# The probabilities of the latent attention turned by VectorE, and its output one group later

## The chip, the cores and the metric

The kernel runs on one core of a Trainium2 chip. The metric is device time in microseconds (us) of one launch. The kernel before takes 2406.18 us, the median of three runs (2406.07 to 2406.28).

## The reference, cut to what matters

Two transformer blocks over a sequence of 256 tokens of width 2048, in float32. The second block has three attention branches (A, B and C); each is multiplied by a SiLU gate, projected to width 2048, multiplied by a sigmoid gate, and the three are summed. The change is in branch B, a latent attention with 8 heads. A head has queries and keys of 192 features (128 plain ones and 64 rotated ones) and values of 128:

```python
logits = jnp.einsum('bthd,bshd->bhts', qb, k) * 192 ** -0.5
logits = jnp.where(causal, logits, -jnp.inf)        # 128 queries at a time
p = jax.nn.softmax(logits, axis=-1)
o_b = jnp.einsum('bhts,bshd->bthd', p, v)           # then times silu(bz)
```

The last product sums over the keys. On TensorE the summed dimension lies on the partitions, so the probabilities, whose partitions are the queries, have to be turned before it. With two blocks of 128 queries and causal masking, a head has three squares of 128x128 probabilities: 384 columns.

## The kernel before, in words

**The weight stream.** All weights come from one stream of 841 groups of 512 KB, two tiles of 128x512 each. A group passes a ring of four slots (`RING`): SyncE's queue loads it into `RAW`, ScalarE copies it to `WH` (the high part, line 1165), VectorE computes `WL = RAW - WH` (the low part, line 1722), and TensorE multiplies it in twelve matmuls of 128x512 (lines 682 to 684): high by high, high by low, low by high, for two tiles and two halves of the tokens. ScalarE's split of group j waits until TensorE has used group j-4 (`group_used`), VectorE's waits for ScalarE's (`hi_split`), TensorE's matmuls wait for VectorE's (`lo_split`), and the load of a slot waits for the low split of the group that was in it.

**Order on an engine.** Each engine runs one list of instructions in order; engines wait for one another by semaphores. The functions named `b_step(i, p)` exist on TensorE, ScalarE and VectorE and say what that engine does for the attention after group p of a merge. ScalarE and VectorE do the split of group p+4 first and then the step of p; with p in `ahead` (ScalarE, line 1341) or a function `first` (VectorE, line 1955), something comes before that split.

**The stage.** `merge_a` runs four times 12 groups: eight of a gate's weights and four of branch A's projection. Beside each 12 groups it computes two heads of branch B, a pair i = 0 to 3. ("Group 5" is group 5 of the twelve; "split 9" the split of group 9, which is issued at step 5.) The steps of a pair are:

- TensorE at step 4: the scores of the pair (`pair_scores`, lines 1082 and 1087), in PSUM banks 6 and 7.
- VectorE at step 4, after split 8: scaled and masked scores `BSC` (line 2363) and the negated maxima (2365, 2366).
- ScalarE at step 5, after split 9: a load of the activation table and four exponentials into `BPR` (1678), with their sums.
- TensorE at step 7: six transposes of `BPR` through the identity into PSUM banks 4 and 5 (`pair_probs`, line 1095). ScalarE at step 7 copies them to `BPT` (1683).
- TensorE at step 8: the values' products from `BPT` (`pair_values`, 1104). VectorE at step 8: the gated rows `BOF` (2369, 2373).
- At step 10: TensorE turns `BOF` (`pair_output`, 1112), ScalarE copies the high part to `U[2]` (1686), VectorE subtracts the low part (2380) and counts `head_out`.
- VectorE at steps 7 to 10, after that step's split: 4, 2, 4 and 2 transposes of 32x384 of the next pair's normed and rotated queries and keys `BQK` into `BQT` (`pair_turn`, 2348), and 2 each at the next pair's steps 0 and 1. The first pair's are done by TensorE.
- ScalarE at step 2, after split 6: two gain scalings of `BQT` (1667, 1668), which release that pair's scores (`qkt_ready`).
- VectorE at step 11: the gated product is multiplied and added to the sum (1974, 1977).
- GpSimd prepares `BQK` of the next pair (lines 640 to 660), from the end of the transposes of `BQK` on.

Branch A's attention runs in the merge before (`merge_c`), one head to six groups. There VectorE turns the probabilities already, with sixteen transposes of 32x96 ahead of the split of the head's group 2 (`probs_turn`, line 1838), and the exponentials are ScalarE's step 1.

Of the kernel before, what the change touches and what calls it, by code (L numbers as in the profile page):

```python
# [25 lines left out]
ACT = mybir.ActivationFunctionType  # L26
# [3 lines left out]
P = 128  # L30
# [13 lines left out]
NCH = D // CH  # L44
# [5 lines left out]
CAUS = 3 * P  # L50
# [21 lines left out]
MOBA0, RET0, C0, A0, B0, HEADS = 0, 8, 12, 16, 24, 28  # L72
# [109 lines left out]
def build(nc, x_in, mem_in, w_stream, params, final_w, pos_pack, constants, out):  # L182
    with ExitStack() as ctx:
# [29 lines left out]
        MERGED = {"merged1": sb("MERGED1", [P, T, D], F32, at_pb), "merged2": sb("MERGED2", [P, T, D], F32, at_pa + 20 * KB)}  # L213
# [46 lines left out]
        BPR = sb("BPR", [P, 2, CAUS], F32, at_sgx + 8 * KB)  # L260
        BPT = sb("BPT", [P, 2, CAUS], F32, at_sgx + 11 * KB)
# [23 lines left out]
        PS = ctx.enter_context(nc.psum_tensor("PS", [P, 8, 512], F32))  # L285
# [20 lines left out]
        ident = con("ident")  # L306
# [53 lines left out]
        probs = sem("probs")  # L360
        probs_scaled = sem("probs_scaled")
        v_copied = sem("v_copied")
        pt_done = sem("pt_done")
        pt_ready = sem("pt_ready")
# [301 lines left out]
        def _(pe):  # L666
# [421 lines left out]
                                        start=False, stop=t == T - 1, skip_group_check=True)  # L1088
                ins.then_inc(scores, 1)

            def pair_probs(H):
                pe.wait_ge(probs, H.count(1))
                for r in range(2):
                    for b in range(3):
                        ins = pe.transpose(PS[:, 4 + r, b * P:(b + 1) * P], BPR[:, r, b * P:(b + 1) * P], ident)
                ins.then_inc(pt_done, 1)

            def pair_values(H, i):
                pe.wait_ge(pt_ready, H.count(1))
                for r in range(2):  # L1100
# [14 lines left out]
            def b_step(i, p):  # L1115
                H = At(B0, i, 1)
                if p == 1 and isinstance(i, int):
                    pair_transpose(H)
                elif p == 4:
                    pair_scores(H)  # L1120
                elif p == 7:
                    pair_probs(H)
                elif p == 8:
                    pair_values(H, i)
                elif p == 10:
                    pair_output(H)
            products("gates_b1", [(GD, HT)], 0)
            products("merge_a", [(GD, HT), (GW, U[1])], 0, b_step)
# [7 lines left out]
            g, n = At(GROUP0["out2"]), At(PROD0["out2"] + NCH - 1)  # L1136
# [19 lines left out]
        def _(act):  # L1156
# [140 lines left out]
            for p in range(GD - 1, 2 * GD):  # L1297
# [7 lines left out]
                if p in (GD, GD + 1):  # L1305
# [4 lines left out]
                    ins = act.activation(JUNK[:, t, :], X[:, t, :], ACT.Square, scale=D ** -0.5, accum_out=XR[:, t:t + 1])  # L1310
# [13 lines left out]
            for a in range(2):  # L1324
                act.activation(ROPE[:, 1, a], ANG[:, 0], ACT.Sin)
                ins = act.activation(ROPE[:, 0, a], ANG[:, 1], ACT.Sin, scale=-1.0, bias=con("hpi"))
# [336 lines left out]
            def b_step(i, p):  # L1663
                H = At(B0, i, 1)
                if p == 2 and not isinstance(i, int):
                    act.wait_ge(qk_tr, H.count(2))
                    act.activation(BQT[:, 0:2, :], BQT[:, 0:2, :], ACT.Copy, scale=par("bqn"))
                    act.activation(BQT[:, 2:4, :], BQT[:, 2:4, :], ACT.Copy, scale=par("bkn")).then_inc(qkt_ready, 1)
                elif p == 2:
                    act.wait_ge(qk_tr, H.count(2))  # L1670
                    act.activation(BQT[:, 0:2, :], PS[:, 4, :].rearrange("p (r s) -> p r s", r=2), ACT.Copy, scale=par("bqn"))
                    act.activation(BQT[:, 2:4, :], PS[:, 5, :].rearrange("p (r s) -> p r s", r=2), ACT.Copy, scale=par("bkn"))
                    act.activation(BQT[:, 4:6, :], PS[:, 6, :].rearrange("p (a s) -> p a s", a=2), ACT.Copy).then_inc(qkt_ready, 1)
                elif p == 5:
                    act.wait_ge(maxima, At(20, i, 1).count(1))
                    for t, cols in enumerate((slice(0, P), slice(P, CAUS))):
                        for r in range(2):
                            ins = act.activation(BPR[:, r, cols], BSC[:, r, cols], ACT.Exp, bias=BNM[:, t, r:r + 1],
                                                 accum_out=BRS[:, t, r:r + 1])
                    ins.then_inc(probs, 1)  # L1680
                elif p == 7:
                    act.wait_ge(pt_done, H.count(1))
                    act.activation(BPT[:], PS[:, 4:6, 0:CAUS], ACT.Copy).then_inc(pt_ready, 1)
                elif p == 10:
                    act.wait_ge(ot_done, H.count(1))
                    act.activation(U[2][:, ds(i * 2, 2), 0, :], PS[:, 7, :].rearrange("p (r s) -> p r s", r=2),
                                   ACT.Copy).then_inc(ot_hi, 1)
            merge("merge_a", NCH, 1, 0, b_step, apart=1)
            act.wait_ge(head_out, HEADS + 1)
            act.dma_start(X[:], rows(x_scratch)).then_inc(x_back, 16)  # L1690
            gates_b("gates_b", 2, 2)
# [22 lines left out]
        def _(dve):  # L1714
# [638 lines left out]
            def b_step(i, p):  # L2353
                H = At(B0, i, 1)
                own, ahead = not (isinstance(i, int) and i == 0), not (isinstance(i, int) and i == NCH - 1)
                if own and p < 2:
                    pair_turn(H, 6 + p)
                if ahead and 7 <= p < 11:
                    for h in ((0, 1), (2,), (3, 4), (5,))[p - 7]:
                        pair_turn(At(B0 + 1, i, 1), h)  # L2360
                if p == 4:
                    dve.wait_ge(scores, H.count(1))
                    link(dve.scalar_tensor_tensor(out=BSC[:], in0=PS[:, 6:8, 0:CAUS], scalar=192 ** -0.5,
                                                  in1=con("mask").unsqueeze(1).broadcast_to([P, 2, CAUS]), op0=ALU.mult, op1=ALU.add))
                    dve.tensor_reduce(BNM[:, 0], BSC[:, :, 0:P], AX_X, ALU.max, negate=True)
                    dve.tensor_reduce(BNM[:, 1], BSC[:, :, P:CAUS], AX_X, ALU.max, negate=True).then_inc(maxima, 1)
                elif p == 8:
                    dve.wait_ge(probs, H.count(1))
                    link(dve.reciprocal(BRI[:], BRS[:]))
                    dve.wait_ge(pv_done, H.count(1))  # L2370
                    for r in range(2):
                        for t in range(T):
                            ins = dve.scalar_tensor_tensor(out=BOF[:, r, t], in0=PS[:, 6, r * S + t * P:r * S + (t + 1) * P],
                                                           scalar=BRI[:, t, r:r + 1], in1=PB[:, t, ds((i * 2 + r) * P + PB_Z, P)],
                                                           op0=ALU.mult, op1=ALU.mult)
                    ins.then_inc(o_rows, 1)
                elif p == 10:
                    dve.wait_ge(ot_hi, H.count(1))
                    u = U[2][:, ds(i * 2, 2)]
                    dve.tensor_tensor(u[:, :, 1, :], PS[:, 7, :].rearrange("p (r s) -> p r s", r=2), u[:, :, 0, :].bitcast(F32),  # L2380
                                      ALU.subtract).then_inc(head_out, 1)
            merge("merge_a", NCH, 1, MERGED["merged2"], 2, b_step, apart=True)
            for p in range(2 * GD):
                split(At(GROUP0["gates_b"]), p + RING)
            dve.wait_ge(prod_free, 2 + PROD0["up_b"])
# [134 lines left out]
```

## Time and profile before

| what | value |
|---|---|
| median of 3 runs | 2406.18 us |
| the profiled execution | 2406.36 us |
| its span, first to last instruction | 2404.5 us |
| TensorE busy | 2397.9 us (100%) |
| VectorE busy | 1837.5 us (76%) |
| ScalarE busy | 1235.8 us (51%) |
| GpSimd busy | 320.2 us (13%) |
| granted TensorE clock | 1.00 |

The stage `merge_a` lies at about 2076 to 2229 us of the span. All rows below are of this one execution; times are us from the span's start. Engines: PE is TensorE, DVE VectorE, ACT ScalarE, POOL GpSimd. L1722 is line 1722 of the kernel. A matmul's duration contains the drain of the array; the next one starts before it ends, so the time that a series takes on the path is read from starts.

### The profile page before, as it was taken

The numbers are of one execution on the slowest core, as the hardware profiler recorded it, in microseconds if no ns is written. First come the engines' busy times: TensorE is split into PE (matmuls) and PEld (weight loads), VectorE is DVE, ScalarE is ACT, GpSimd is POOL, SyncE is SP. The second block draws the span as 40 slices with busy tenths as digits, with TensorE's granted clock in tenths as the row PEclk, the third lists the DMA queues.
The fourth block names the chain that finished last, engine by engine and source line by source line (L and its number), as shares of the span: only waits on it lengthen the run. The fifth ranks groups of instructions, "written<-read, shape, count | busy, mean of one in ns | idle before, by whom it ended". The sixth has DMA issues, their size and how long they took to land.

```text
span 2404.5 us, 34078 instructions
## 1 busy us (share of the span) xinstructions
PE 2397.9 (100%) x10821; PEld 1983.1 (82%) x10821; DVE 1837.5 (76%) x2616; ACT 1235.8 (51%) x1585; POOL 320.2 (13%) x277
## 2 busy tenths in 40 slices
PE   9999999999999999999999999999999999999999
PEld 7888888888888888888888888888888888888887
DVE  5467679897888988988888897667767876587584
ACT  5445455555455444444444455455557555655443
POOL 0021242234210000000000000011100000521050
PEclk9999999999999999999999999999999999999999
DMA  7555555576655655555565656855554555555655
GB/s 272 193 186 178 178 177 175 184 245 226 228 185 185 203 196 192 191 193 191 185 199 192 198 188 213 253 184 187 171 187 161 182 166 180 179 167 167 227 193 166
DMA packets 134828, 464.25 MB, mean 193 GB/s; under 512 B 14545, under 2 KB 21329, under 8 KB 134113
## 3 DMA queue, kind: packets, MB, share of 16 engines
q1 hardware_dynamic: 122464, 443.08, 56.2%
q10 hardware_dynamic: 12256, 20.15, 2.7%
q8 instruction: 45, 0.74, 0.1%
q14 instruction: 31, 0.25, 0.0%
q0 software_dynamic: 32, 0.03, 0.0%
HBM read 455.87 MB, written 7.34 MB: 193 GB/s over the span
## 4 chain that ended last, share of the span: by engine, by line
PE 96%; DVE 2%; issue 1%; ACT 1%; DVEq 0%; ACTq 0%
PE PS L682 21%; PE PS L684 21%; PE PS L683 21%; PE PS L929 7%; PE PS L930 7%; PE PS L931 7%; PE PS L949 3%; PE PS L951 3%; PE PS L950 3%; DVE WL L1722 1%; DVE PT L1838 1%; PE PS L798 1%; PE PS L767 1%; PE PS L723 0%; PE PS L1104 0%
## 5 line engine op out<-in xcount | busy, mean ns | idle before, releaser
L1165 ACT ACTIVATE WH<-RAW 128x1024 fp32r<-128x1024 f32 x841 | 889.6, 1061 | 1087.1 <-PE PS L684 693.8
L1722 DVE TENSOR_TENSOR WL<-RAW,WH 128x1024 fp32r<-128x1024 f32 x811 | 1020.7, 1267 | 485.9 <-ACT WH L1165 475.5
L682 PE MATMUL PS<-WH,HT 128*128 128x512 f32 (+1 forms) x1816 | 716.0, 394 | 0.3 <-DVE WL L1722 0.2
L684 PE MATMUL PS<-WH,HT 128*128 128x512 f32 (+1 forms) x1816 | 706.2, 389 | 0.0
L683 PE MATMUL PS<-WL,HT 128*128 128x512 f32 (+1 forms) x1816 | 705.5, 388 | 0.0
L682 PEld LDWEIGHTS PS<-WH,HT 128*128 128x128 f32 x1816 | 341.1, 188 | 71.9 <-issue 3.7
L684 PEld LDWEIGHTS PS<-WH,HT 128*128 128x128 f32 x1816 | 340.9, 188 | 70.9
L683 PEld LDWEIGHTS PS<-WL,HT 128*128 128x128 f32 x1816 | 341.2, 188 | 67.8
L929 PE MATMUL PS<-WH,HT 128*128 128x512 f32 x704 | 274.0, 389 | 0.0
L931 PE MATMUL PS<-WH,HT 128*128 128x512 f32 x704 | 273.9, 389 | 0.0
L930 PE MATMUL PS<-WL,HT 128*128 128x512 f32 x704 | 273.9, 389 | 0.0
L2119 DVE STREAM_TRANSPOSE FU<-PS 32x256 f32<-32x256 f32 x352 | 156.9, 446 | 6.0
L931 PEld LDWEIGHTS PS<-WH,HT 128*128 128x128 f32 x704 | 132.1, 188 | 27.5
L929 PEld LDWEIGHTS PS<-WH,HT 128*128 128x128 f32 x704 | 132.1, 188 | 27.4
L930 PEld LDWEIGHTS PS<-WL,HT 128*128 128x128 f32 x704 | 132.1, 188 | 27.4
L949 PE MATMUL PS<-WH,ACTT 128*128 128x512 f32 x352 | 136.9, 389 | 0.0
L950 PE MATMUL PS<-WL,ACTT 128*128 128x512 f32 x352 | 136.9, 389 | 0.0
L951 PE MATMUL PS<-WH,ACTT 128*128 128x512 f32 x352 | 136.9, 389 | 0.0
L682 PE MATMUL PS<-WH,U 128*128 128x512 f32 x320 | 127.7, 399 | 0.0
L684 PE MATMUL PS<-WH,U 128*128 128x512 f32 x320 | 124.8, 390 | 0.0
L683 PE MATMUL PS<-WL,U 128*128 128x512 f32 x320 | 124.5, 389 | 0.0
L488 POOL TENSOR_TENSOR MS<-MS,CONST 128x4 f32<-128x4 f32 (+1 forms) x6 | 1.2, 200 | 916.8 <-ACT PS L1206 744.3
(320 smaller groups left out, 2328.4 us busy)
## 6 DMA issues: line engine op xcount, KB each, us to landing
RAW<-w_stream SPq DMA_DIRECT2D x841, 512.0 KB, 3.4
bias_scratch<-BE ACTq DMA_DIRECT2D x12, 256.0 KB, 4.1
MEMR<-mem_in ACTq DMA_DIRECT2D x1, 2048.0 KB, 10.8
X<-x_in ACTq DMA_DIRECT2D x4, 512.0 KB, 4.3
x_scratch<-X ACTq DMA_DIRECT2D x4, 512.0 KB, 4.4
X<-x_scratch ACTq DMA_DIRECT2D x1, 2048.0 KB, 11.7
out<-X ACTq DMA_DIRECT2D x8, 256.0 KB, 3.2
X<-x_in SPq DMA_DIRECT2D x3, 512.0 KB, 9.9
```

What stands on the lines that cost most here:

```text
L682: pe.matmul(o, hi, WH[:, slot, kk, 0:cols], start=k == 0, stop=False)
L683: pe.matmul(o, hi, WL[:, slot, kk, 0:cols], start=False, stop=False)
L684: ins = pe.matmul(o, lo, WH[:, slot, kk, 0:cols], start=False, stop=k == nq * GK - 1)
L929: pe.matmul(o, hi, WH[:, slot, kk, :], start=k == 0, stop=False)
L930: pe.matmul(o, hi, WL[:, slot, kk, :], start=False, stop=False)
L931: ins = pe.matmul(o, lo, WH[:, slot, kk, :], start=False, stop=k == KT - 1)
L949: pe.matmul(o, hi, WH[:, slot, kk, :], start=k == 0, stop=False)
L950: pe.matmul(o, hi, WL[:, slot, kk, :], start=False, stop=False)
L951: ins = pe.matmul(o, lo, WH[:, slot, kk, :], start=False, stop=k == FT - 1)
L1165: act.activation(WH[:, g.slot(j)], RAW[:, g.slot(j)], ACT.Copy).then_inc(hi_split, 1)
L1722: dve.tensor_tensor(WL[:, s], RAW[:, s], WH[:, s].bitcast(F32), ALU.subtract).then_inc(lo_split, 1)
L2119: ins = dve.transpose(dst, src)
```

## The change: what it does

For each pair of heads the six TensorE transposes of the probabilities and ScalarE's copy of them go. VectorE turns the probabilities instead, from `BPR` straight to `BPT`, in sixteen transposes of 32x192 (32 partitions by six blocks of 32) ahead of its split of step 5 (that of group 9). On ScalarE the exponentials of step 5 stand ahead of that step's split. The output's three parts move from step 10 to step 11. TensorE adds one to the semaphore `pt_done` after the scores, so that its count stays right.

```diff
--- before.py
+++ after.py
@@ -1088,13 +1088,6 @@
                                         start=False, stop=t == T - 1, skip_group_check=True)
                 ins.then_inc(scores, 1)
 
-            def pair_probs(H):
-                pe.wait_ge(probs, H.count(1))
-                for r in range(2):
-                    for b in range(3):
-                        ins = pe.transpose(PS[:, 4 + r, b * P:(b + 1) * P], BPR[:, r, b * P:(b + 1) * P], ident)
-                ins.then_inc(pt_done, 1)
-
             def pair_values(H, i):
                 pe.wait_ge(pt_ready, H.count(1))
                 for r in range(2):
@@ -1118,11 +1111,10 @@
                     pair_transpose(H)
                 elif p == 4:
                     pair_scores(H)
-                elif p == 7:
-                    pair_probs(H)
+                    pe.sem_inc(pt_done, 1)
                 elif p == 8:
                     pair_values(H, i)
-                elif p == 10:
+                elif p == 11:
                     pair_output(H)
             products("gates_b1", [(GD, HT)], 0)
             products("merge_a", [(GD, HT), (GW, U[1])], 0, b_step)
@@ -1678,14 +1670,11 @@
                             ins = act.activation(BPR[:, r, cols], BSC[:, r, cols], ACT.Exp, bias=BNM[:, t, r:r + 1],
                                                  accum_out=BRS[:, t, r:r + 1])
                     ins.then_inc(probs, 1)
-                elif p == 7:
-                    act.wait_ge(pt_done, H.count(1))
-                    act.activation(BPT[:], PS[:, 4:6, 0:CAUS], ACT.Copy).then_inc(pt_ready, 1)
-                elif p == 10:
+                elif p == 11:
                     act.wait_ge(ot_done, H.count(1))
                     act.activation(U[2][:, ds(i * 2, 2), 0, :], PS[:, 7, :].rearrange("p (r s) -> p r s", r=2),
                                    ACT.Copy).then_inc(ot_hi, 1)
-            merge("merge_a", NCH, 1, 0, b_step, apart=1)
+            merge("merge_a", NCH, 1, 0, b_step, apart=1, ahead=(5,))
             act.wait_ge(head_out, HEADS + 1)
             act.dma_start(X[:], rows(x_scratch)).then_inc(x_back, 16)
             gates_b("gates_b", 2, 2)
@@ -2374,12 +2363,23 @@
                                                            scalar=BRI[:, t, r:r + 1], in1=PB[:, t, ds((i * 2 + r) * P + PB_Z, P)],
                                                            op0=ALU.mult, op1=ALU.mult)
                     ins.then_inc(o_rows, 1)
-                elif p == 10:
+                elif p == 11:
                     dve.wait_ge(ot_hi, H.count(1))
                     u = U[2][:, ds(i * 2, 2)]
                     dve.tensor_tensor(u[:, :, 1, :], PS[:, 7, :].rearrange("p (r s) -> p r s", r=2), u[:, :, 0, :].bitcast(F32),
                                       ALU.subtract).then_inc(head_out, 1)
-            merge("merge_a", NCH, 1, MERGED["merged2"], 2, b_step, apart=True)
+
+            def b_turn(i, p):
+                H = At(B0, i, 1)
+                if p == 5:
+                    dve.wait_ge(probs, H.count(1))
+                    for a in range(4):
+                        for b in range(4):
+                            src = BPR[32 * a:32 * a + 32].rearrange("p r (n s) -> p (r n) s", s=P)[:, :, 32 * b:32 * b + 32]
+                            dst = BPT[32 * b:32 * b + 32].rearrange("p r (n s) -> p (r n) s", s=P)[:, :, 32 * a:32 * a + 32]
+                            ins = dve.transpose(dst, src)
+                    ins.then_inc(pt_ready, 1)
+            merge("merge_a", NCH, 1, MERGED["merged2"], 2, b_step, apart=True, first=b_turn)
             for p in range(2 * GD):
                 split(At(GROUP0["gates_b"]), p + RING)
             dve.wait_ge(prod_free, 2 + PROD0["up_b"])
```

## Rows read from the trace of the kernel before

**Rows 1.** Busy time in 38 us of the second pair: us of each engine (instructions), clock, DMA

```profile
core 0: us, PE busy (x) PEld busy (x) DVE busy (x) ACT busy (x) POOL busy (x), PEclk, DMA share, GB/s
2116.00:2154.00 38.00, 38.00 (x186) 31.36 (x185) 30.76 (x40) 20.46 (x28) 12.47 (x11) 1.00 0.51 168
```

**Rows 2.** Timeline of TensorE: start, us, engine, line, tiles, count; second to fourth pair

```profile
2127.03 1.47 PE L1082 MATMUL PS<-BQT 128*128 128x128 f32 x8
...
2141.01 1.50 PE L1104 MATMUL PS<-KVB,BPT 128*128 x12
...
2164.62 1.47 PE L1082 MATMUL PS<-BQT 128*128 128x128 f32 x8
...
2202.21 1.47 PE L1082 MATMUL PS<-BQT 128*128 128x128 f32 x8
```

**Rows 3.** Chain of waits that ended last: start, us, engine and line; second pair

```profile
2137.77 0.66 PE PS L1095 x6
```

**Rows 4.** Groups by line and shape: VectorE's transposes, busy us and mean ns

```profile
L1838 DVE STREAM_TRANSPOSE PT<-PR 32x96 f32<-32x96 f32 x128 | 34.5, 269 | 2.7 <-ACT PR L1248 1.1
L1850 DVE STREAM_TRANSPOSE OFT<-OF 32x128 f32<-32x128 f32 x112 | 33.9, 303 | 1.8
L1946 DVE STREAM_TRANSPOSE QKT<-QK 32x256 f32<-32x256 f32 x64 | 27.9, 435 | 1.0
```

**Rows 5.** Timeline of VectorE in the merge before (branch A)

```profile
1959.22 0.41 DVE L1790 TENSOR_REDUCE NM<-SC 128x1 f32<-128x256 f32 x1
...
1961.05 4.51 DVE L1838 STREAM_TRANSPOSE PT<-PR 32x96 f32<-32x96 f32 x16 [0.29 <-ACT PR L1248]
1965.60 3.50 DVE L1722 TENSOR_TENSOR WL<-RAW,WH 128x1024 fp32r<-128x1024 f32 x3
```

**Rows 6.** Timeline of VectorE, second pair to the start of the fourth

```profile
2122.84 1.16 DVE L2348 STREAM_TRANSPOSE BQT<-BQK 32x384 f32<-32x384 f32 x2
...
2126.37 1.46 DVE L1722 TENSOR_TENSOR WL<-RAW,WH 128x1024 fp32r<-128x1024 f32 x1 [1.10 <-ACT WH L1165]
2128.32 1.50 DVE L1722 TENSOR_TENSOR WL<-RAW,WH 128x1024 fp32r<-128x1024 f32 x1 [0.49 <-ACT WH L1165]
2129.74 0.95 DVE L2363 SCALAR_TENSOR_TENSOR BSC<-PS,CONST 128x768 f32<-128x768 f32 x1
...
2131.05 0.68 DVE L2366 TENSOR_REDUCE BNM<-BSC 128x2 f32<-128x512 f32 x1
...
2140.17 2.31 DVE L2348 STREAM_TRANSPOSE BQT<-BQK 32x384 f32<-32x384 f32 x4
2142.88 1.23 DVE L1722 TENSOR_TENSOR WL<-RAW,WH 128x1024 fp32r<-128x1024 f32 x1 [0.40 <-ACT WH L1165]
...
2160.60 1.16 DVE L2348 STREAM_TRANSPOSE BQT<-BQK 32x384 f32<-32x384 f32 x2
...
2198.19 1.16 DVE L2348 STREAM_TRANSPOSE BQT<-BQK 32x384 f32<-32x384 f32 x2
```

**Rows 7.** Timeline of ScalarE, second pair

```profile
2124.68 0.71 ACT L1668 ACTIVATE BQT<-BQT,PARAM 128x512 f32<-128x512 f32 x1
...
2133.44 1.28 ACT L1678 ACT_TABLE_LOAD   x1
2134.74 0.40 ACT L1678 ACTIVATE BPR<-BSC,BNM 128x128 f32<-128x128 f32 x1
...
2136.42 0.19 ACT L1678 ACTIVATION_READ_ACCUMULATOR BPR<-BSC,BNM 128x1 f32 x1
```

**Rows 8.** Timeline of ScalarE in the merge before (branch A)

```profile
1958.73 1.28 ACT L1247 ACT_TABLE_LOAD   x1
```

**Rows 9.** Timeline of VectorE, first pair

```profile
2093.41 0.68 DVE L2366 TENSOR_REDUCE BNM<-BSC 128x2 f32<-128x512 f32 x1
...
2105.37 1.22 DVE L1722 TENSOR_TENSOR WL<-RAW,WH 128x1024 fp32r<-128x1024 f32 x1 [0.54 <-ACT WH L1165]
```

**Rows 10.** Timeline of VectorE in the first block's retention

```profile
361.29 2.51 DVE L1850 STREAM_TRANSPOSE OFT<-OF 32x128 f32<-32x128 f32 x8
```

**Rows 11.** Timeline of GpSimd at the same time

```profile
361.25 0.74 POOL L541 TENSOR_TENSOR JK<-PA,CONST 128x256 f32<-128x256 f32 x1 [0.18 <-POOL QK L540]
```

## The prediction

> **What bounds the kernel now.** I read the busy times by stretch first. In the second pair of heads [rows 1] TensorE is busy for all of its 38 us at a granted clock of 1.00 and VectorE for 30.8 us. So TensorE sets the end, and VectorE has only 7.2 us left. Then I read TensorE's timeline for its period: the score products of the second, third and fourth pair start at 2127.03, 2164.62 and 2202.21 us [rows 2], a round of 37.59 us, and no wait stands between them. Last I read VectorE's and ScalarE's timelines of the second pair for the order of their work. Both run in order, and the change puts new work into that order, so what it costs depends on how far ahead of TensorE they are at each step, more than on busy shares.
>
> **What is removed from TensorE.** The six transposes of the probabilities take 0.66 us of the chain of waits in the second pair [rows 3]; the other three pairs have 0.65 or 0.66. Four times 0.65 is 2.6 us on the path. ScalarE's copy of them out of PSUM goes too; ScalarE is busy for 20.5 of 38 us [rows 1], so that is worth nothing by itself. The bare semaphore step that takes the transposes' place costs between 0 and 0.1 us a pair; I take 0.
>
> **What is added to VectorE.** Sixteen transposes of 32x192 a pair, a shape that this trace lacks. Its neighbours are 32x128 at 303 ns and 32x256 at 435 ns [rows 4]: halfway is about 370 ns. Sixteen of 32x96 (269 ns each) last 4.51 us from first start to last end [rows 5], so the pitch is (4.51-0.27)/15 = 0.283, 0.013 over the duration. I take 15 x 0.383 + 0.37 = 6.11 us. The ends are those of the neighbours: 15 x 0.316 + 0.30 = 5.04 and 15 x 0.448 + 0.44 = 7.16 us.
>
> The Trainium skill (VectorE: DVE Perf Modes, The three transpose paths) would have it otherwise: it gives a 128x128 bf16 transpose as 311 ns on VectorE and 390 ns on TensorE. By that the six squares of a pair would cost VectorE an estimated 1.9 us. The trace disagrees for this fp32 form: three squares take 4.51 us on VectorE [rows 5], and six take 0.66 us of TensorE's path [rows 3].
>
> **What the transposes wait for, and what waits behind them.** They wait for the exponentials, and the low parts of groups 9, 10 and 11 stand behind them, then the next pair's key and query transposes. Let T be the end of the last of these transposes (a pair's sub-step 1): 2124.00 for the second pair, 2161.76 for the third, 2199.35 for the fourth [rows 6]. After T come ScalarE's two gain scalings, done 1.39 us later (2125.39) [rows 7], and only then TensorE's score products. They started 1.64 us after the scalings were done: that is all the lead there is.
>
> VectorE's round from T to T, second pair:
> - T to the start of low split 7: 2.37 us, as now (ScalarE scales, then splits). From there to low split 8: now 1.95; ScalarE will no longer wait for TensorE before its split 8, so VectorE goes straight on at about 1.37 (its 1.46 us less the usual overlap of 0.09). Low split 8 to the scaled scores 1.42, to the end of the maxima 1.99 [rows 6]. Sum 7.15; now 7.73.
> - Maxima to the end of the exponentials: 2136.42 + 0.19 - 2134.74 = 1.87 [rows 7], with 0.03 to start, 1.90. The activation table's load (1.28 us, now after split 9) I take as hidden: ahead of the group it can run while ScalarE waits for the maxima, as it does in the merge of the branch before, where the load starts at 1958.73 [rows 8] and the maxima end at 1959.63 [rows 5].
> - The sixteen transposes, 0.03 + 6.11 = 6.14.
> - Low splits 9, 10, 11: three in a row last 3.50 us, a pitch of (3.50-1.22)/2 = 1.14 [rows 5]; with 0.03 ahead and 1.25 for the last (its 1.23 and a start), 3.56. Their high halves are ready by then: ScalarE has the time of the transposes for them.
> - Four transposes for the next pair, 2.31, to the start of split 12, 2.33 [rows 6].
>
> From the maxima's end to the start of split 12 that is 1.90 + 6.14 + 3.56 + 2.33 = 13.93 us, against 2142.88 - 2131.73 = 11.15 now: VectorE's present waits in that stretch hide most of the 8 us, not all. From split 12 to T nothing changes in sum (2161.76 - 2142.88 = 18.88; the lower half of the output stands one group later in the same queue). The round becomes 7.15 + 13.93 + 18.88 = 39.96 us, now 37.76. TensorE's own becomes 37.59 - 0.65 = 36.94.
>
> **The output one group later.** TensorE's four transposes, ScalarE's copy and VectorE's subtraction move together. At group 10 TensorE would have to wait for the gated rows; at 11 they are about ready. Queued behind are only ScalarE's and VectorE's next splits, two groups or more ahead of TensorE, and after the fourth pair the load of x, which is wanted a stage later. I take 0; its ends are what the round already contains.
>
> **The sum.** First pair: no transposes of its own wait ahead of its scores, so nothing changes up to its maxima, which end at 2094.09. Split 12 then starts at 2094.09 + 13.93 = 2108.02, now 2105.37 [rows 9]: 2.65 later. T of the second pair is 2126.65, its scores start 1.39 + 0.05 later, at 2128.1; TensorE could be there at 2127.03 - 0.65 = 2126.4. It waits 1.7 us. Second and third pair: TensorE waits 39.96 - 36.94 = 3.0 each, most of it ahead of the score products, the rest ahead of the values and the output. Fourth pair: nothing is turned for a next one. Its transposes end 6.6 (2.37 + 2 x 1.14 + 1.99, T to maxima with no GpSimd work beside it) + 1.90 + 6.14 = 14.7 us after T. TensorE reaches the values 1.44 + (2141.01 - 2127.03) - 0.65 = 14.8 us after T [rows 2]. No wait, but no lead. So 1.7 + 3.0 + 3.0 - 2.6 = +5.1 us. The profiled execution was 2406.36 us (span 2404.5 and 1.9 around it), which gives 2411.5; it is 0.18 above the median of 2406.18. I forecast 2411.4.
>
> With transposes of 5.04 us each of three rounds is 1.07 shorter: +1.9, 2408.2. With 7.16 each is 1.05 longer and the fourth pair waits 1.0 for its values: +9.3, 2415.6.
>
> **Rivals.**
> - *All hidden, not slower.* VectorE's sixteen transposes disappear in its idle 7.2 us, as the same step of the branch before does (4.51 us, and no TensorE wait in the trace). Then only the 2.6 us count: 2403.6. The place is the score products. It decides at the length of the transposes: at 3.1 us (0.19 us each) the round fits into 36.94 and nearly everything is gained; at 4.4 us (0.27 each, the price of a 32x96) gain and waits are equal. Against it: the shape is twice as wide, and the branch before has no next pair's transposes in the queue. By the Trainium skill's figure above, the 1.9 us, this rival would win.
> - *The table load isn't hidden.* Today it stands between split 9 and the exponentials [rows 7]. If it runs only once the maxima are there, each of three rounds is 1.28 longer and the fourth pair's values wait 1.3: 2411.4 + 5.1 = 2416.5. Against it: [rows 5, 8].
> - *GpSimd stretches the transposes.* It prepares the next pair beside them. Low split 7 lasts 1.46 us beside it, split 12 without it 1.23 [rows 6]. Some 4 us of the second and third pair's transposes lie beside GpSimd: stretched by 0.19 that is 0.8 in two rounds, 2413.0. Against it: eight 32x128 transposes beside a GpSimd multiplication take 2.51 us, 0.314 each [rows 10], no more than their duration and the usual 0.013; the multiplication is that of [rows 11].
>
> **How the numbers follow.** My case 0.72, own range 2409.5 to 2413.5 (a third of the way to the ends of the transposes' cost); all hidden 0.14; table load 0.06; GpSimd 0.08. The range runs from 2406.5 to 2415.5: it takes in the transposes' ends, and leaves out the full gain and the full table load. 0.2% is 4.8 us, about what a measurement of this kernel can tell from no change: faster means under 2401.4, slower over 2411.0. No case is under 2403.6, so faster keeps 0.03 for what I have not seen. My case lies just above the line, at 0.58 of its chance: 0.72 x 0.58 = 0.42, with the two worse rivals 0.56 for slower. The rest, 0.41, is no change.
>
> **What would show it.** Right: the transposes' line has 64 instructions of about 370 ns; TensorE waits ahead of the score products of the second, third and fourth pair, released by ScalarE's gain scaling, about 1.7, 2 and 2 us, and the scores start near 2128.1, 2168.1 and 2208.1; after the fourth pair no wait; the probabilities' transposes are gone from the chain and VectorE and ScalarE appear in it in this stage. The load of the table starts before the maxima end. Wrong: score products 36.9 us apart without a wait (all hidden), transposes of 32x192 much off 370 ns, or waits ahead of ordinary groups, which would mean that the low splits are late, not the key and query transposes.

## The result, and the profile after

The changed kernel takes 2412.53 us (median of nine runs, 2412.30 to 2414.06), the kernel before 2406.28 (nine runs, 2406.07 to 2406.37): a ratio of 1.0028, with a 95% interval of 1.0019 to 1.0036. It is 6.2 us slower. The forecast was 2411.4. The profiled execution of the changed kernel is one of the longer ones: 2414.06 us, with a span of 2412.3 and a mean granted clock of 0.999.

Busy times of the same 38 us as in [rows 1], after the change (the columns are those of [rows 1]):

```profile
2116.00:2154.00 38.00, 35.60 (x169) 28.57 (x168) 34.16 (x53) 19.21 (x26) 11.51 (x11) 1.00 0.46 153
```

TensorE, which had no gap in this stretch, now stands idle for 2.4 us of it, and VectorE is busy for 34.2 us instead of 30.8. What TensorE waits for in this stage (from 2080 to 2240 us; engine, tile and line that waited, what released it: us in total, times, longest):

```profile
engine line waited for: us in total, times, longest us
PE PS L1082 <- ACT BQT L1660: 5.2, 3, 1.9
PE PS L1097 <- DVE BPT L2380: 1.9, 2, 0.9
```

Before the change this view is empty in the same stretch. L1082 are the score products, L1660 is ScalarE's second gain scaling; L1097 are the products with the values, L2380 VectorE's transposes. TensorE's timeline, to be laid beside [rows 2]:

```profile
2128.06 1.58 PE L1082 MATMUL PS<-BQT 128*128 128x128 f32 x8 [1.46 <-ACT BQT L1660]
...
2142.56 1.60 PE L1097 MATMUL PS<-KVB,BPT 128*128 x12 [0.94 <-DVE BPT L2380]
...
2168.48 1.58 PE L1082 MATMUL PS<-BQT 128*128 128x128 f32 x8 [1.86 <-ACT BQT L1660]
...
2208.91 2.62 PE L1082 MATMUL PS<-BQT 128*128 128x128 f32 x8 [1.90 <-ACT BQT L1660]
2211.46 1.50 PE L1087 MATMUL PS<-BQT 64*128 64x128 f32 x8
2212.89 0.50 PE L682 MATMUL PS<-WH,HT 128*128 128x512 f32 x1
...
2223.91 1.50 PE L1097 MATMUL PS<-KVB,BPT 128*128 x12
```

The score products start 1.03, 3.86 and 6.70 us later than in [rows 2], 40.42 and 40.43 us apart instead of 37.59: 2.8 us are lost in each round. The values of the fourth pair (last line) wait for nothing.

VectorE's timeline of the second pair, to be laid beside [rows 6], with the fourth pair's splits below:

```profile
2125.48 1.16 DVE L2337 STREAM_TRANSPOSE BQT<-BQK 32x384 f32<-32x384 f32 x2
...
2128.98 3.45 DVE L1711 TENSOR_TENSOR WL<-RAW,WH 128x1024 fp32r<-128x1024 f32 x2 [1.09 <-ACT WH L1157]
2132.36 0.94 DVE L2352 SCALAR_TENSOR_TENSOR BSC<-PS,CONST 128x768 f32<-128x768 f32 x1
...
2133.67 0.68 DVE L2355 TENSOR_REDUCE BNM<-BSC 128x2 f32<-128x512 f32 x1
2136.28 6.13 DVE L2380 STREAM_TRANSPOSE BPT<-BPR 32x192 f32<-32x192 f32 x16 [1.93 <-ACT BPR L1670]
2142.44 3.50 DVE L1711 TENSOR_TENSOR WL<-RAW,WH 128x1024 fp32r<-128x1024 f32 x3
...
2148.17 1.22 DVE L1711 TENSOR_TENSOR WL<-RAW,WH 128x1024 fp32r<-128x1024 f32 x1
...
2165.90 1.16 DVE L2337 STREAM_TRANSPOSE BQT<-BQK 32x384 f32<-32x384 f32 x2
...
2209.84 2.36 DVE L1711 TENSOR_TENSOR WL<-RAW,WH 128x1024 fp32r<-128x1024 f32 x2 [1.09 <-ACT WH L1157]
```

From the maxima to split 12 VectorE has only the 1.93 us of the exponentials free. T, the end of a pair's last key and query transposes, is 2126.64 for the second pair and 2167.06 for the third: a round of 40.42 us, TensorE's new period. ScalarE in the first and the second pair, beside [rows 7]:

```profile
2090.87 1.28 ACT L1670 ACT_TABLE_LOAD   x1
2094.21 0.40 ACT L1670 ACTIVATE BPR<-BSC,BNM 128x128 f32<-128x128 f32 x1 [2.06 <-DVE BNM L2355]
...
2129.92 1.28 ACT L1670 ACT_TABLE_LOAD   x1
2134.38 0.40 ACT L1670 ACTIVATE BPR<-BSC,BNM 128x128 f32<-128x128 f32 x1 [3.18 <-DVE BNM L2355]
```

The table load is over 2 to 3 us before the maxima are there, and costs nothing.

One thing more is in this execution. The fourth pair's score products last 2.62 and 1.50 us, 3.98 from their first start to the start of the next group (2208.91 to 2212.89). The third pair's, also behind a wait, take 2.37 (2168.48 to 2170.85). The windows around them (columns as above; the third pair's first) show why:

```profile
2168.00:2170.00 2.00, 1.52 (x10) 1.14 (x10) 0.91 (x2) 2.00 (x3) 2.00 (x3) 1.00 0.58 205
...
2208.00:2210.00 2.00, 1.09 (x4) 0.96 (x5) 0.91 (x2) 2.00 (x4) 0.00 (x0) 0.82 0.56 201
2210.00:2212.00 2.00, 2.00 (x9) 1.30 (x9) 2.00 (x2) 1.98 (x2) 0.00 (x0) 0.50 0.65 244
2212.00:2214.00 2.00, 2.00 (x13) 1.32 (x10) 1.15 (x2) 0.05 (x1) 0.00 (x0) 0.83 0.78 279
```

The granted clock, 1.00 up to 2208, falls to 0.50, 1.2 of 2.4 GHz, behind the wait of 1.90 us, and comes back after 2212. Behind the third pair's wait of 1.86 us it stayed at 1.00. The fall costs 3.98 - 2.37 = 1.6 us, and it accounts for the distance of this execution from the six shorter ones (2412.30 to 2412.57, so 2414.06 - 2412.5 = 1.6). The Trainium skill (TensorE: Matmul & The Clock Gate, Why this matters for your kernels) warns that idle gaps between bursts of matmuls bring half rate. The row agrees on the level; the gap here, 1.90 us, is shorter than those that the page warns of.

### The profile page after: what moved, and what is told of

Read it like the earlier page. It is cut to its first block, busy times and chain, and to the rows that moved or that the text cites. A ratio compares the mean times of both kernels' runs of the same rounds, so it can differ in the third digit from the quotient of the medians.

```text
span 2412.3 us, 34094 instructions
## 1 busy us (share of the span) xinstructions
PE 2398.7 (99%) x10797; PEld 1981.4 (82%) x10797; DVE 1860.3 (77%) x2680; ACT 1231.5 (51%) x1581; POOL 319.0 (13%) x277
## 4 chain that ended last, share of the span: by engine, by line
PE 91%; DVE 5%; issue 2%; ACT 1%; DMA 0%; DVEq 0%; ACTq 0%; SPq 0%
PE PS L682 19%; PE PS L684 19%; PE PS L683 19%; PE PS L931 7%; PE PS L930 7%; PE PS L929 7%; PE PS L951 3%; PE PS L950 3%; PE PS L949 3%; DVE WL L1711 2%; DVE BQT L2337 1%; DVE PT L1827 1%; DVE BPT L2380 1%; PE PS L798 1%; PE PS L767 1%
```

## The experiments

The theory, A: VectorE's queue sets the round, in the order exponentials, sixteen transposes, splits 9 to 11, next pair's turns, next scores. The rivals: B, TensorE's waits come from single steps, each with its own price; C, the time comes from the move of the output or of the exponentials; D, which comes from the trace above, that part of the time is the clock behind the waits. In all diffs a removed line is the changed kernel's.

**The output back at group 10**, in the steps of TensorE, ScalarE and VectorE.

```diff
-                elif p == 11:
+                elif p == 10:
```

> The changed kernel with the output's three parts back at step 10. Theory A (VectorE's round sets the time: exponentials, sixteen transposes, splits 9 to 11 and the next pair's transposes stand in one queue ahead of the next score products): TensorE now waits some 2 us for the gated rows at step 10 of the first three pairs, but its wait ahead of the next score products shrinks by as much, since VectorE's round of 40.4 us is the same. Score products at 2128, 2168.5 and 2209 as in the changed kernel, 2412.4 us, within 0.6 of the changed kernel's 2412.5. Rival B (the waits add up, TensorE's own place of the output matters): three waits of 2 us more, 2418.5. Rival C (moving the output by a group is what costs the time): back towards 2404 to 2407.

Measured: 2415.05 us (2412.74 to 2415.58, six runs), ratio 1.0035 [1.0022, 1.0048]. T stayed at 2126.5, as A says, but the total missed A's number by 2.6. TensorE now waits at the output, 2.0 to 2.3 us, and after it runs at half speed (timeline of TensorE, first pair):

```profile
2111.69 0.73 PE L1105 MATMUL PS<-CONST,BOF 128*128 128x128 f32 x4 [2.02 <-DVE BOF L2362]
...
2113.08 0.63 PE L684 MATMUL PS<-WH,U 128*128 128x512 f32 x1
2113.50 0.63 PE L682 MATMUL PS<-WH,U 128*128 128x512 f32 x1
```

The matmuls are 0.43 us apart, where they are 0.23 at full clock. The one run of the six with a mean clock of 1.00 took 2412.74, within 0.4 of A's number. So C fell for the output, and D was put to the test below.

**The exponentials not ahead.**

```diff
-            merge("merge_a", NCH, 1, 0, b_step, apart=1, ahead=(5,))
+            merge("merge_a", NCH, 1, 0, b_step, apart=1)
```

> The changed kernel with the exponentials behind ScalarE's split 9 again, as in the kernel before. Theory A: the table load (1.28) is no longer hidden and in the first pair split 9's wait for TensorE is added: exponentials start 3.0 us after the maxima's end in the first pair (now 0.03), about 1.35 in the later ones; these lengthen VectorE's round, and in the fourth pair the values wait 1.3. 3.0 + 1.35 + 1.35 + 1.3 = +7, 2419.5 us. Rival B (the low splits or TensorE's removed work set the time, ScalarE has time to spare): within 1 us of 2412.5.

Measured: 2423.97 us (2422.45 to 2425.44, four runs), ratio 1.0072 [1.0055, 1.0089]. ScalarE now makes its split of group 9 first and loads the table after it (timelines of ScalarE, then of VectorE, first pair):

```profile
2094.38 1.06 ACT L1157 ACTIVATE WH<-RAW 128x1024 fp32r<-128x1024 f32 x1 [4.08 <-PE PS L684]
2095.46 1.28 ACT L1670 ACT_TABLE_LOAD   x1
2096.75 0.40 ACT L1670 ACTIVATE BPR<-BSC,BNM 128x128 f32<-128x128 f32 x1
```

```profile
2098.65 4.57 DVE L2380 STREAM_TRANSPOSE BPT<-BPR 32x192 f32<-32x192 f32 x12 [5.02 <-ACT BPR L1670]
```

VectorE stands 5.02 us ahead of the first pair's transposes instead of 1.93, and the whole 3.1 us goes into the first round, as A says. The total is 4.5 above A's number. Part of that is the clock, which falls behind some of the waits (mean 0.997 to 0.998); the last experiment shows how much.

**No transposes at all.** This kernel leaves out the turning of the probabilities; the values take them as they are.

```diff
-                pe.wait_ge(pt_ready, H.count(1))
+                pe.wait_ge(probs, H.count(1))
...
-            merge("merge_a", NCH, 1, MERGED["merged2"], 2, b_step, apart=True, first=b_turn)
+            merge("merge_a", NCH, 1, MERGED["merged2"], 2, b_step, apart=True)
```

> The changed kernel without any turning of the probabilities: the values' products read the unturned ones, so the output isn't the reference's. Theory A: VectorE's round is 40.4 - 6.1 = 34.3 us, shorter than TensorE's own 36.9; no wait ahead of any score product, these 36.9 us apart, and the whole saving of the six TensorE transposes is seen: 2406.3 - 2.6 = 2403.7 us. Rival C (the output's move or the exponentials' place costs by itself): 2406 or more, with waits left at the score products.

Measured: 2403.43 us (2403.08 to 2403.62, ten runs), ratio 0.9988 [0.9979, 0.9998]. Score products on TensorE:

```profile
2126.35 1.47 PE L1082 MATMUL PS<-BQT 128*128 128x128 f32 x8
2163.25 1.47 PE L1082 MATMUL PS<-BQT 128*128 128x128 f32 x8
2200.13 1.47 PE L1082 MATMUL PS<-BQT 128*128 128x128 f32 x8
```

36.9 us apart and no wait: this is TensorE's own period, and what the rival "all hidden" would have looked like. The gain on TensorE is real, 2.9 us, and the transposes cost 9.1 (2412.53 - 2403.43). C fell: everything else of the change is in this kernel too.

**Eight more transposes.** They go into an idle tile, behind the sixteen, after TensorE has been told that the probabilities are turned.

```diff
                     ins.then_inc(pt_ready, 1)
+                    again = TMP[:].rearrange("p t n -> p (t n)")[:, 0:2 * CAUS]
+                    for a in range(2):
+                        for b in range(4):
...
+                            dve.transpose(dst, src)
```

> The changed kernel with eight more transposes of 32x192 (into an idle tile) right behind the sixteen, after these have released the values: 3.06 us more on VectorE a pair. Theory A: three rounds are 3.06 longer each, and in the fourth pair low split 9 comes 2.9 us too late for TensorE: 9.2 + 2.9 = +12.1, 2424.6 us; score products about 43.5 us apart. Rival B (what counts is that the values wait for the turned probabilities; what follows is hidden by the ring's lead of four groups): +0 to +3, 2412.5 to 2415.5.

Measured: 2425.28 us (2424.03 to 2425.86, four runs), ratio 1.0078 [1.0061, 1.0094]. The eight last 3.04 us, and the round grows by as much: scores at 2131.05, 2174.52 and 2218.00, 43.5 us apart. Nobody waits for these eight, so B, by which only the length of what is waited for counts (2412.5 to 2415.5), fell here. The waits moved, too (waits of TensorE from 2080 to 2240 us):

```profile
PE PS L682 <- DVE WL L1711: 10.1, 4, 2.6
```

Most of the time is now lost at ordinary groups, whose low parts stand behind the transposes; the clock falls here too (mean 0.998), so that the total holds more than VectorE's round.

**Filler matmuls in the wait.** Six matmuls into a PSUM bank that nobody reads, ahead of the score products' wait, from the second pair on.

```diff
+                for _ in range(0 if isinstance(H.i, int) and H.i == 0 else 6):
+                    pe.matmul(PS[:, 5, :], U[1][:, 0, 0, 0:P], U[1][:, 0, :, :], start=True, stop=True)
```

> The changed kernel with six more matmuls of 128x512 on TensorE ahead of its wait for the score products of the second to fourth pair, into a PSUM bank that nobody reads (1.36 us of the 1.7 to 2.1 us that it waits there). Theory A: VectorE's round is untouched, so nothing is lost: 2412.4 us. Theory D, on top of A (in the profiled execution of the changed kernel the clock falls to 0.50 behind the last of these waits and costs 1.7 us, in others it doesn't): with TensorE busy up to 0.4 to 0.8 us before the score products the clock stays at 1.00, all executions lie within 0.6 us of 2412.4 and none at 2414. Rival (the slower executions have another cause): the spread stays, 2412.3 to 2414.1; or six matmuls add 4 us.

Measured: 2412.25 us (2412.12 to 2412.58, ten runs, mean clock 1.00 in each), ratio 1.0025 [1.0015, 1.0035]. Without the fillers three of nine runs took over 2413.4. Waits of TensorE, and the fourth pair's scores and values:

```profile
PE PS L1099 <- DVE BPT L2382: 1.9, 2, 0.9
PE PS L1084 <- ACT BQT L1662: 1.0, 2, 0.5
```

```profile
2208.84 1.58 PE L1084 MATMUL PS<-BQT 128*128 128x128 f32 x8 [0.49 <-ACT BQT L1662]
...
2222.24 1.60 PE L1099 MATMUL PS<-KVB,BPT 128*128 x12
```

The scores start when they did without fillers (2208.91), and run at full speed; the median is the same within 0.3 us. So the waits are VectorE's doing, and the fall of the clock is the second, smaller cost that some executions pay on top (D). Three runs of nine against none of ten is thin evidence for D by itself; the last two experiments repeat it.

**One head by each engine.** VectorE turns the first head's three squares (sixteen 32x96), TensorE and ScalarE's copy the second's, as before.

```diff
-                            src = BPR[32 * a:32 * a + 32].rearrange("p r (n s) -> p (r n) s", s=P)[:, :, 32 * b:32 * b + 32]
+                            src = BPR[32 * a:32 * a + 32, 0].rearrange("p (n s) -> p n s", s=P)[:, :, 32 * b:32 * b + 32]
...
+                for b in range(3):
+                    ins = pe.transpose(PS[:, 5, b * P:(b + 1) * P], BPR[:, 1, b * P:(b + 1) * P], ident)
```

> The changed kernel with only one head of each pair turned by VectorE (sixteen transposes of 32x96, 4.51 us in branch A's merge), the other by three TensorE transposes at step 7 and a copy by ScalarE. Theory A: VectorE's round 40.4 - 1.6 = 38.8 us, TensorE's own 36.94 + 0.33 = 37.27: no wait in the second pair, 1.5 in the third and fourth, 4 x 0.32 saved: 2406.3 + 3.1 - 1.3 = 2408.1 us. Rival (each step that TensorE gives up is a gain of its own, VectorE has room for one head): 2405.0.

Measured: 2407.83 us (2407.52 to 2408.00, ten runs), ratio 1.0006 [0.9997, 1.0016]. Scores on TensorE:

```profile
2126.80 1.47 PE L1083 MATMUL PS<-BQT 128*128 128x128 f32 x8
2165.26 1.58 PE L1083 MATMUL PS<-BQT 128*128 128x128 f32 x8 [1.05 <-ACT BQT L1669]
2204.08 1.58 PE L1083 MATMUL PS<-BQT 128*128 128x128 f32 x8 [1.30 <-ACT BQT L1669]
```

That is A's number (2408.1) and not the rival's (2405.0). With the kernels above, VectorE's time for the transposes of one pair orders the totals: 0, 4.5, 6.1 and 9.2 us give 2403.4, 2407.8, 2412.3 (clock held) and 2425.3 (clock not held).

**Three splits of each round to GpSimd.** The transposes stay. GpSimd, which is done with its preparation by 2139.7 us, makes the low parts of groups 11, 13 and 15.

```diff
+        POOL_AT = (7, 9, 11)
...
+                low_splits_of(At(GROUP0["merge_a"], i, GD + GW), [p + RING for p in POOL_AT])
...
-                        split(g, p + RING)
+                        if not (add and p in POOL_AT):
+                            if add and (p - 1) % per in POOL_AT:
+                                dve.wait_ge(lo_split, g.count(p + RING))
+                            split(g, p + RING)
...
```

> The changed kernel with the low splits of groups 11, 13 and 15 of each round given to GpSimd, which is idle from 13 us after T on. Theory A: three splits of 1.14 to 1.25 leave VectorE's round, some 0.5 comes back as a wait for GpSimd's split 11: 40.4 - 3.1 = 37.3 us against TensorE's own 36.9; no wait in the second pair, about 0.4 in the third and fourth: 2406.3 - 2.6 + 0.8 = 2404.5 us (2404.0 to 2405.5), and no fall of the clock. Rival (the sixteen transposes cost through what waits for them directly, the values and splits 9 and 10, not through the length of the round): 2411 to 2412.5.

Measured: 2404.13 us (2403.79 to 2404.26, ten runs, mean clock 1.00), ratio 0.9990 [0.9981, 1.0000]. The interval reaches 1.0000, but all ten lie under all 31 runs of the kernel before beside them (2406.01 to 2407.89). VectorE and GpSimd in the second pair:

```profile
2132.83 6.12 DVE L2393 STREAM_TRANSPOSE BPT<-BPR 32x192 f32<-32x192 f32 x16 [1.94 <-ACT BPR L1680]
...
2141.26 2.31 DVE L2350 STREAM_TRANSPOSE BQT<-BQK 32x384 f32<-32x384 f32 x4
2144.05 1.23 DVE L1721 TENSOR_TENSOR WL<-RAW,WH 128x1024 fp32r<-128x1024 f32 x1 [0.48 <-POOL WL L580]
```

```profile
2141.53 2.40 POOL L580 TENSOR_TENSOR WL<-RAW,WH 128x1024 fp32r<-128x1024 f32 x1 [5.28 <-DVE WL L1721]
```

The waits ahead of the scores are gone (one of 0.2 us is left ahead of the third pair's values), with all sixteen transposes still in place: the queue was the cause, not the transposes' own length. This version beats both kernels, by 8.4 and 2.2 us.

**The same splits in the kernel before.** The control: GpSimd's three splits, but the probabilities turned by TensorE, the exponentials and the output where they were. Against the kernel before:

```diff
...
+                low_splits_of(At(GROUP0["merge_a"], i, GD + GW), [p + RING for p in POOL_AT])
...
```

> Control: the kernel before with the same three low splits given to GpSimd. Theory A: VectorE's round isn't the bound there, so nothing is gained: 2406.3 us within 0.4. Rival (GpSimd's help is a gain by itself): 2404 to 2405.5.

Measured: 2406.43 us (2406.08 to 2406.57, ten runs), ratio 1.0000 [0.9991, 1.0010]. Where VectorE doesn't set the round, relieving it gives nothing; the 2.2 us are TensorE's removed transposes.

**GpSimd later.** The round was 0.46 us over the forecast, and the place was splits 7 and 8, beside GpSimd's preparation of the next pair. Here that preparation is held until the maxima are done (with the six fillers).

```diff
+                hold(maxima, At(20, i, 1).count())
...
```

> The kernel with six filling matmuls (2412.25 us) with GpSimd's preparation of the next pair begun only after the maxima, so that it no longer lies beside low splits 7 and 8. The rounds of 40.4 us were 0.5 longer than forecast, and these two splits took 3.38 us to the scaled scores where I had 2.79. Theory A2 (GpSimd beside them stretches these two splits): they take 2.3 to 2.4 us, each of two rounds is 1.0 shorter there; against it GpSimd then lies beside splits 9 to 11 (up to 0.6 longer together) and may hold up the next pair's transposes (up to 1.4): 2411 to 2414 us in all. Rival (the two are slow because they follow directly on each other, or on ScalarE's splits): they still take 3.4.

Measured: 2413.93 us (2413.62 to 2414.10, six runs, mean clock 1.00), ratio 1.0032 [1.0019, 1.0044]. VectorE and GpSimd in the second pair:

```profile
2129.82 2.36 DVE L1714 TENSOR_TENSOR WL<-RAW,WH 128x1024 fp32r<-128x1024 f32 x2 [1.09 <-ACT WH L1160]
...
2142.17 4.79 DVE L1714 TENSOR_TENSOR WL<-RAW,WH 128x1024 fp32r<-128x1024 f32 x3
```

```profile
2134.38 1.04 POOL L649 TENSOR_TENSOR BQK<-QB,MST 128x512 f32 x1 [28.88 <-DVE BNM L2358]
...
2142.69 1.50 POOL L501 TENSOR_TENSOR BQK<-BQK,JK 128x256 f32<-128x256 f32 x1 [0.18 <-POOL BQK L500]
```

Splits 7 and 8 fall from 3.45 to 2.36 us, so GpSimd had stretched them. But now its last instructions lie beside splits 9 to 11, which grow from 3.50 to 4.79: the cost moves, and the round (T from 2127.47 to 2168.09, 40.62) doesn't shrink. The first pair's splits 9 to 11 are stretched as well (4.78), so its round grows too, and the total is 1.7 us longer than with the fillers alone.

**The output at group 10, with fillers.** The first experiment with four filler matmuls ahead of the output's wait.

```diff
+                for _ in range(4):
+                    pe.matmul(PS[:, 5, :], U[1][:, 0, 0, 0:P], U[1][:, 0, :, :], start=True, stop=True)
...
+                elif p == 10:
```

> The output at step 10 once more, with four more matmuls of 128x512 (0.91 us) ahead of TensorE's wait for the gated rows, into a bank that nobody reads. Theory A with the clock's fall (D): the first run's 2415 was the clock at half speed behind each wait of 2.0 to 2.3 us; with 1.1 to 1.4 us left of each wait the clock stays at 1.00, the waits only change place, and the four matmuls cost 0.9 in the fourth pair, which has no wait there: 2412.3 + 0.9 = 2413.2 us, no execution over 2413.8. Rival B (waits add up by themselves): 2415 and more.

Measured: 2413.47 us (2413.10 to 2415.26, six runs, mean clock 1.00 in each), ratio 1.0031 [1.0019, 1.0044]. Five runs are within 0.4 of the expectation; the sixth, 2415.26, is not, and its cause stays open. The scores, at 2128.09, 2168.40 and 2208.80, start where they do in the changed kernel. In the fourth pair TensorE waits for nothing at the output, and the fillers cost their own 0.9 us there, as expected:

```profile
2228.88 1.07 PE L1103 MATMUL PS<-U 128*128 128x512 f32 x4
2229.79 0.60 PE L1107 MATMUL PS<-CONST,BOF 128*128 128x128 f32 x4
```

So of the 1.2 us over the kernel with six fillers (2413.47 - 2412.25) 0.9 are the fillers', and the output's move is worth some 0.3 us. The first experiment's run at a clock of 1.00 says the same (2412.74 beside 2412.5). The other 2.3 us that the first experiment lost (2415.05 - 2412.74) were the clock.

**The exponentials behind, with fillers.** The second experiment with six fillers ahead of the scores and four ahead of the values.

```diff
+                for _ in range(0 if isinstance(H.i, int) and H.i == 0 else 6):
+                    pe.matmul(PS[:, 5, :], U[1][:, 0, 0, 0:P], U[1][:, 0, :, :], start=True, stop=True)
...
+            merge("merge_a", NCH, 1, 0, b_step, apart=1)
```

> The exponentials behind split 9 once more, with six filling matmuls ahead of the wait for the scores and four ahead of the wait for the turned probabilities. Theory A with D: the first run's 2424 was 4 to 5 us of half clock. Without it: exponentials 3.1 us after the maxima in the first pair (scores 2.6 later), 1.4 later than in the changed kernel in the next two, 2.5 in the fourth: 2412.25 + 2.6 + 1.4 + 1.4 + 2.5 = 2420.1 us, clock 1.00. Rival (the excess is a wait of its own): 2423 to 2424 again.

Measured: 2421.08 us (2420.64 to 2421.24, four runs, mean clock 1.00), ratio 1.0061 [1.0045, 1.0078]; 1.0 above A's number, and under D's rival. Against 2412.25 the exponentials ahead of ScalarE's split are worth 8.8 us to the change; the clock made the other 2.9 of the second experiment's loss (2423.97 - 2421.08). The fillers cost nothing here, since TensorE still waits 0.5 and 1.5 us behind them. Part of the 2.9 went through ScalarE: its split of group 9 waits for TensorE, and with the clock at 0.50 it came so late in the second pair that VectorE stood 5.02 us ahead of its transposes, where it stands 3.42 with the clock held.

## Why the prediction was right

The direction, the mechanism and the size held: 2411.4 forecast, 2412.53 measured, inside the range. (The forecast's own sum, 2411.5 for the profiled execution, less the 0.18 by which that lies over the median, is 2411.3 and not 2411.4.) Step by step:

- *TensorE's saving.* 2.6 us forecast; the kernel without any transposes gained 2.9.
- *The shape that the trace lacked.* 370 ns forecast; 64 instructions with a median of 370 ns, sixteen in 6.12 us (6.11 forecast). The halfway point between two neighbours was the right choice, and the wide range not needed.
- *What stands behind them.* Maxima to split 12: 13.93 forecast, 2148.17 - 2134.35 = 13.82 measured (the maxima end at 2133.67 + 0.68). T of the second pair: 2126.65 and 2126.64. Scores: 2128.1 and 2128.06.
- *The table load hidden*, and *GpSimd doesn't stretch the transposes*: both rivals fell. GpSimd works until 2139.7, beside 3.4 us of the second pair's transposes; they take 6.13, the first pair's without it 6.12.
- *The fourth pair's values.* No wait, no lead: its transposes end at 2215.97 + 6.12 = 2222.09 in the kernel with fillers, and TensorE takes them at 2222.24.
- *All hidden* fell; its price was right. The figure of the Trainium skill by which it would have won (VectorE: DVE Perf Modes, The three transpose paths) doesn't hold for this fp32 form: 6.12 us for six squares, an estimated 1.9 by the page.

The term that was mis-sized is the way from low split 7 over low split 8 to the scaled scores: 1.37 and 1.42 us, 2.79 in sum. It measured 2132.36 - 2128.98 = 3.38. The first part held (1.39); the second took 1.99, because split 8 itself lasted 2.06 us instead of the 1.50 of [rows 6]. I had taken its time from before, when ScalarE's wait held it back to 4.32 us after T, and one of GpSimd's products was nearly over. Now it starts 3.73 us after T and lies beside a longer part of that product, and beside the next one (VectorE's line, then GpSimd's):

```profile
2130.37 2.06 DVE L1711 TENSOR_TENSOR WL<-RAW,WH 128x1024 fp32r<-128x1024 f32 x1
```

```profile
2129.33 2.02 POOL L651 TENSOR_TENSOR BQK<-KVB,MST 128x512 f32 x1
2131.31 1.59 POOL L653 TENSOR_TENSOR BQK<-PB,MST 128x256 f32<-128x256 f32 x1
```

That GpSimd is the cause is shown by the experiment that held it back: without it beside them, both splits together take 2.36 us instead of 3.45.

So the round is 40.42 and not 39.96 (+0.59 here, -0.11 from the maxima to split 12, the rest within 0.03), and each of the third and fourth pair waits 40.42 - 36.94 = 3.5, not 3.0. The second pair's wait was 1.6 us, not 1.7. The sum becomes 1.6 + 3.5 + 3.5 - 2.6 = +6.0 us: 2406.36 + 6.0 = 2412.4, what the six shorter executions took (2412.30 to 2412.57). The view of waits shows only 7.1 of these 8.6 us: the last matmul before a wait is credited with 0.39 us where the next would have come after 0.23, and the first group after one lasts 0.1 longer (1.58 for 1.47), some 0.26 for each of five waits. The prediction named "1.7, 2 and 2" for the scores' waits; 1.46, 1.86 and 1.90 are that, less 0.16.

What the prediction lacked altogether is the clock. A wait of 1.9 us can cost more than its length: 1.6 us more in the profiled execution. The median escaped it because six of the nine executions were not lengthened so; why one execution of the same kernel is and another isn't stays open. Waits of about 2 us were forecast; with the output at group 10, waits of 2.0 to 2.3 us lengthened five of six executions. That the median came out near the forecast with the clock left out is in part luck.

## What to carry to other kernels

An engine with 20% of idle time has no room for work of 16% if the work stands in an in-order queue ahead of what the bounding engine needs next: add up that queue from one hand-over to the next, and compare this round with the bounding engine's own. To move work off the bounding engine, first move something else out of that queue, here three splits to GpSimd, without which the same change costs 6 us and with which it gains 2. When TensorE has waits like those here (falls of the clock were seen behind waits of 1.9 to 2.6 us), reckon with the clock too, and test it with matmuls that nobody reads.

## What the runs showed of the hardware

- TensorE's clock fell to 0.50 behind waits of 1.90 us (the changed kernel) to 2.61 us (the kernel with eight more transposes), and matmuls 0.23 us apart were then 0.43 apart. The length of the wait alone did not decide: with the exponentials not ahead, the values of the second and of the third pair waited 2.42 us each in one execution, and the clock was at 0.51 in the 2 us from the start of the former and at 1.00 from the start of the latter. No fall was seen behind waits up to 1.86 us. Six filler matmuls kept the mean at 1.00 in all ten runs.
- VectorE's splits, which read two tiles in SBUF, and GpSimd's products stretch each other: two splits 2.36 us alone, 3.45 beside GpSimd; a GpSimd product of 128x512 1.04 alone or beside VectorE's transposes, 1.86 to 2.02 beside the splits. Not every split loses: the one that began at 2126.67 us, ahead of the product of 1.86 us (from 2126.93), kept its 1.22. Transposes, which read one tile, are untouched (6.12 and 6.13 us). The Trainium skill (GPSIMD Engine Reference, Key points) says that GpSimd shares its SBUF interfaces with VectorE and contends with instructions that have two SBUF inputs. The rows agree, and add the price.
- ScalarE loads its activation table ahead of the wait of the instruction that needs it: the load starts at 2090.87, the maxima for which that instruction waits end at 2094.18.
